# The first feed-forward of a two-model kernel: tile pairs as seven block products in three parts, late modulation units moved to the down parts

## The reference

```python
def swiglu(h, w1, w2):
    gate, up = jnp.split(h @ w1, 2, axis=-1)
    return (jax.nn.silu(gate) * up) @ w2
...
    cond = jax.nn.silu(c)
    for layer in range(DEPTH):
        mod = cond @ ada_w[layer] + ada_b[layer]
        sh1, sc1, g1, sh2, sc2, g2 = jnp.split(mod, 6, axis=-1)
        ...
        h = modulate(rms_norm(x, ffn_norm[layer]), sh2, sc2)
        x = x + g2[:, None, :] * swiglu(h, ffn_w1[layer], ffn_w2[layer])
```

## Time and profile before

| | |
|---|---|
| median of 3 runs | 2526.47 us (2524.81 to 2528.64) |
| the profiled execution's own time | 2526.73 us |
| its span | 2524.7 us |
| mean granted TensorE clock | 0.992 of full speed |
| TensorE, matmuls | 2465.2 us, 98% |
| GpSimd | 1787.9 us, 71% |
| VectorE | 1144.8 us, 45% |
| ScalarE | 542.3 us, 21% |
| first layer's feed-forward, from its first raw tile to the next layer's first shift rows | 362.57 to 740.01 us |
| second layer's, the same stretch | 937.16 to 1293.27 us |

### The profile page before, as it was taken

The page is one execution under the profiler, slowest core; times in us unless marked ns, Lnnn a source line. Parts: engine busy times, 40 slices in busy tenths (PEclk is TensorE's granted clock), DMA queues, the critical chain, the costliest instruction groups (busy, mean ns, idle before and its releaser), DMA issues.

```text
span 2524.7 us, 34103 instructions
## 1 busy us (share of the span) xinstructions
PE 2465.2 (98%) x12183; PEld 1997.5 (79%) x12183; DVE 1144.8 (45%) x2070; ACT 542.3 (21%) x1091; POOL 1787.9 (71%) x1519
## 2 busy tenths in 40 slices
PE   6999999999999999999999999999999999999998
PEld 3677778888887768898988778788878888888886
DVE  5897756444337448363570223105664124331322
ACT  3213520000012522151511011113443101100100
POOL 5564367788887457767798755786555988888885
PEclk9999999999999999999999999999999999999999
DMA  6323225555532122232342211221112222222222
GB/s 260 125 75 134 75 100 178 188 182 173 195 104 75 47 68 92 99 109 93 107 159 97 84 59 59 84 92 67 59 51 101 93 98 92 93 98 100 92 100 83
DMA packets 73376, 267.64 MB, mean 106 GB/s; under 512 B 8240, under 2 KB 9024, under 8 KB 72768
## 3 DMA queue, kind: packets, MB, share of 16 engines
q1 hardware_dynamic: 60288, 215.97, 25.3%
q10 hardware_dynamic: 12992, 50.34, 5.8%
HBM read 262.08 MB, written 4.19 MB: 105 GB/s over the span
## 4 chain that ended last, share of the span: by engine, by line
PE 88%; DVE 6%; POOL 2%; ACT 1%; DMA 1%; issue 1%; ACTq 0%; DVEq 0%; SPq 0%; POOLq 0%
PE ps L444 22%; PE ps L445 22%; PE ps L446 22%; PE ps L845 2%; PE ps L849 2%; PE ps L848 2%; PE ps L675 2%; PE ps L676 2%; PE ps L677 2%; PE ps L1278 1%; PE ps L696 1%; PE ps L1334 1%; POOL lowers L2195 1%; DMA ring<-in_stream 1%; PE ps L1359 1%
## 5 line engine op out<-in xcount | busy, mean ns | idle before, releaser
L2192 POOL TENSOR_TENSOR uppers<-ring,ones 128x512 fp32r<-128x512 f32 x714 | 758.2, 1062 | 562.6 <-DMA ring<-in_stream 558.6
L2195 POOL TENSOR_TENSOR lowers<-ring,uppers 128x512 fp32r<-128x512 f32 x714 | 937.9, 1314 | 55.9
L444 PE MATMUL ps<-x_hi,uppers 128*128 128x512 f32 x864 | 351.5, 407 | 0.0
L446 PE MATMUL ps<-x_hi,lowers 128*128 128x512 f32 x864 | 337.3, 390 | 0.0
L445 PE MATMUL ps<-x_lo,uppers 128*128 128x512 f32 x864 | 337.0, 390 | 0.0
L444 PE MATMUL ps<-h_hi,uppers 128*128 128x264 f32 (+1 forms) x832 | 285.7, 343 | 4.0 <-DVE od_lo L3146 3.4
L445 PE MATMUL ps<-h_lo,uppers 128*128 128x264 f32 (+1 forms) x832 | 279.6, 336 | 0.0
L446 PE MATMUL ps<-h_hi,lowers 128*128 128x264 f32 (+1 forms) x832 | 278.8, 335 | 0.0
L445 PE MATMUL ps<-hid,uppers 128*128 128x512 f32 x704 | 274.3, 390 | 0.0
L444 PE MATMUL ps<-hid,uppers 128*128 128x512 f32 x672 | 263.0, 391 | 0.0
L446 PE MATMUL ps<-hid,lowers 128*128 128x512 f32 x672 | 261.6, 389 | 0.0
(11 more groups left out here) (432 smaller groups left out, 4180.9 us busy)
## 6 DMA issues: line engine op xcount, KB each, us to landing
ring<-in_stream SPq DMA_DIRECT2D x389, 512.0 KB, 3.2
sq<-in_ada_late ACTq DMA_DIRECT2D x20, 512.0 KB, 3.2
rs<-in_ada_late ACTq DMA_DIRECT2D x20, 512.0 KB, 4.7
big<-in_ada_late ACTq DMA_DIRECT2D x16, 512.0 KB, 4.3
big<-in_stream SPq DMA_DIRECT2D x13, 512.0 KB, 16.0
gate<-in_ada_rest ACTq DMA_DIRECT2D x12, 512.0 KB, 3.2
big<-in_ada_rest ACTq DMA_DIRECT2D x12, 512.0 KB, 3.8
hbuf<-in_stream SPq DMA_DIRECT2D x4, 512.0 KB, 6.8
```

Of the source, the lines that this page charges most:

```text
L444: pe.matmul(out, upper, hi, start=start, stop=False)
L446: return pe.matmul(out, lower, hi, start=False, stop=stop)
L2192: pool.tensor_tensor(uppers[:, s, at], w[:, at], ones[:, 0:1].broadcast_to((P, UNIT // 2)), ALU.mult)\
L2195: pool.tensor_tensor(lowers[:, s, at], w[:, at], uppers[:, s, at].bitcast(F32), ALU.subtract)\
```

## The change

The first layer gets the second's form: `ffn` goes on all engines, and `ffn1` takes a layer. All 40 late units move out of the up stage: groups 0 to 4 stand between the residuals of down part a, groups 5 to 9 between those of part b. Their sums stand behind down tiles 1, 2, 4, 5 and 6 of these parts. Their loads are issued by ScalarE as one stretch of 20 ahead of `first_weights` of the next run. Late and last units use the same two buffers in `big`. The four last groups stay ahead of residuals 0 to 3 and their sums behind tiles 1 to 4, now of part c. The second raw operand of f0 and of the next norm moves to other memory; the wait for the last tile's first unit goes, the raw splits stay together ahead of residual 7.

```diff
-        late_w = [sq, rs]
+        LATE0 = 20 * S
...
+        PLAIN = 3
-        HIDDEN_AT = {"f0": 0, "f1": FF}
+        HIDDEN_AT = {"f0": 0, "f1": 2 * PLAIN}
...
+        def late0(k):
+
+            return late_hi[:, k, :], late0_lo[:, k, :]
...
+        LATE_GROUPS = ((0, 1), (2, 3, 4), (5, 6, 7, 8, 9))
+        LATE_SUM_BEHIND = (1, 2, 4, 5, 6)
...
-        last_w = [big[:, TAIL + n * UNIT:TAIL + (n + 1) * UNIT].rearrange("p (a b) -> p a b", b=S) for n in (1, 2)]
+        late_w = last_w = [big[:, TAIL + n * UNIT:TAIL + (n + 1) * UNIT].rearrange("p (a b) -> p a b", b=S) for n in (1, 2)]
...
# TensorE
             def late_sum(i):
+                if i in (0, 2, 5):
+                    claim(7, ("late", [g[0] for g in LATE_GROUPS].index(i)), True)
                 pe.wait_ge(sem("late_read1"), i * 2 + 2)
...
-            def down_part(st, pack, part):
+            def down_part(st, pack, part, behind=None):
...
+                if behind is None:
+                    with pe.Fori(0, 2) as i:
+                        for q in range(4):
+                            tile(i, q)
+                else:
+                    for n in range(KC):
+                        tile(n // 4, n % 4)
+                        behind(n)
+
+            def late_behind(n, first):
+
+                if n in LATE_SUM_BEHIND:
+                    late_sum(first + LATE_SUM_BEHIND.index(n))
+
+            def last_behind(n):
+
+                if 1 <= n <= ADA_LAST:
+                    if n == 1:
+                        claim(7, "late2", True)
+                    ada_sum("last", n - 1, C("chunk_carry"), ps[:, 7, (n - 1) * NT:n * NT])
+
+            def ffn1(st, layer):
+
+                w1, w2 = f"w1_{layer}", f"w2_{layer}"
+                early, late, last = (lambda n: late_behind(n, 0), lambda n: late_behind(n, 5), last_behind) if layer == 0 else 3 * [None]
...
                 seven_products(st, KC - 2 * PLAIN)
-                down_part("f1a", "w2_1", 0)
+                down_part(st + "a", w2, 0, early)
...
-            ffn("f0", 0)
+            ffn1("f0", 0)
...
# ScalarE
+            def late_loads(first, count):
+
+                for unit in range(first, first + count):
+                    if unit >= 2:
+                        act.wait_ge(sem(f"late_read{unit % 2}"), unit // 2)
+                    late_load(unit, unit % 2)
+
             def ffn1(st):
...
                 for run in (1, 2):
+                    if st == "f0":
+                        late_loads(5 * ADA_UNITS * (run - 1), 5 * ADA_UNITS)
                     first_weights(st, run)
                     seven_run(st, run, 0)
...
# VectorE
             def residual(...):
                 for k in range(KC):
+                    if before is not None:
+                        before(k)
                     if between is not None and k == KC - 1:
                         between()
...
-                    if k == KC - 1 and held is not None:
-                        dve.wait_ge(emptied[held % RING], held // RING + 1)
+                    if k == KC - 1 and held:
                         for n in range(KC - 1):
                             raw_split(st, n, *raw(n))
...
+            def late_out(n):
+
+                first, count = LATE_GROUPS[n][0], len(LATE_GROUPS[n])
+                a, at = (ADA_FIRST + ADA_REST + first) * NT, first * NT
+                dve.wait_ge(sem("late_sum_free"), first + count + 1)
+                drain_link(tt(mod[:, a:a + count * NT], ps[:, 7, at:at + count * NT], V("ada_b", a, count * NT), ALU.add), ("late", n))
+
+            def early_groups(k):
+
+                if k == 0:
+                    late_group(0)
+                    late_group(1)
+                    late_out(0)
+                elif 3 <= k < 6:
+                    late_group(k - 1)
+                elif k == 6:
+                    late_out(1)
+
+            def late_groups(k):
+
+                if k in (0, 1, 2, 4, 5):
+                    late_group(5 + (0, 1, 2, 4, 5).index(k))
+                elif k == 6:
+                    late_out(2)
...
+                for run, part, groups in ((1, "a", early_groups), (2, "b", late_groups)):
+                    residual(st + part, None, layer, 5, between=lambda: first_weights(st, run), before=groups if layer == 0 else None)
                     seven_run(st, run, 0)
...
-            residual("f0", "n1", 0, 5, raw=lambda k: (late_hi[:, k, :], late_lo[:, k, :]), held=last_tile["f0"], last=True)
+            residual("f0c", "n1", 0, 5, raw=late0, held=True, last=True)
```

More of the change, by code:

```diff
@@ L783, in late_sum @@
                 mm.then_inc(sem("late_sum_free"), 1)
[L785 to L831, removed]
@@ L900, in down_part, with tile @@
                 done = state["pairs"]
-                with pe.Fori(0, 2) as i:
-                    for q in range(4):
+                def tile(i, q, first=True):
                         take(i, q)
@@ L934, in ffn1 @@
                 seven_products(st, KC - 2 * PLAIN)
-                down_part("f1a", "w2_1", 0)
-                stream("w1_1", 2 * KC, 2 * KC)
+                down_part(st + "a", w2, 0, early)
+                stream(w1, 2 * KC, 2 * KC)
                 seven_products(st, KC)
-                down_part("f1b", "w2_1", 1)
-                stream("w1_1", 4 * KC, 2 * PARTS[2])
+                down_part(st + "b", w2, 1, late)
+                stream(w1, 4 * KC, 2 * PARTS[2])
                 seven_products(st, PARTS[2])
[L941 to L947, removed]
+                if layer == 1:
+                    claim(7, "meta_ss")
+                    pe.wait_ge(sem("meta_squared"), 1)
+                    for k in range(KC):
+                        mm = pe.matmul(ps[:, 7, 0:META], ones[:, :], sq[:, 0, k * META:(k + 1) * META],
+                                       start=k == 0, stop=k == KC - 1)
+                    mm.then_inc(full[7], 1)
+                down_part(st + "c", w2, 2, last)
             def first_mix_out():
@@ L1200, in _ @@
             first_mix_out()
[L1201 to L1205 removed]
+            ffn1("f0", 0)
             stream("cd", 0, 4)
[L1208 removed]
+            raw_tiles("n1", [("u", t) for t in range(4)], late0, True)
             for x in range(2):
@@ L1676, in shift_rows, with ffn_pass @@
                     drain(f(bias_rows[:, p, :], ps[0:2, b, 0:2 * P], ACT.Copy), b)
-            def ffn_pass(st, i, late=0, pairs=(0, 1)):
+            def ffn_pass(st, i, pairs=(0, 1)):
                 if type(i) is int and i == 0:
@@ L2321, in sum_square, with residual @@
                 ins.then_inc(sem("x_summed"), 1)
-            def residual(y, st, layer=None, part=0, raw=None, held=None, rs2=False, last=False, between=None):
+            def residual(y, st, layer=None, part=0, raw=None, held=False, rs2=False, last=False, between=None, before=None):
                 for k in range(KC):
+                    if before is not None:
+                        before(k)
                     if between is not None and k == KC - 1:
@@ L2351, in residual @@
                         continue
-                    if raw is not None and (held is None or k == KC - 1):
+                    if raw is not None and (not held or k == KC - 1):
                         raw_split(st, k, *raw(k))
@@ L2543, in first_pass @@
-            def first_pass(st, late, hid=hid, kept=False):
+            def first_pass(st, hid, kept):
                 layer = 0 if st == "f0" else 1
@@ L2575, in first_pass, with ffn_pass @@
                     normalise(st, k, x_hi[:, k, :], x_lo[:, k, :], coef, shift, kept)
[L2576 to L2579, removed]
                 pair(1)
-                if late:
-                    late_unit(0, 2)
-                    late_unit(0, 3)
-            def ffn_pass(st, i, late, hid=hid, pairs=(0, 1)):
+            def ffn_pass(st, i, hid, pairs=(0, 1)):
                 for p in pairs:
```

77 lines of the change are left out of this document (31 added, 46 removed).

## The result

The changed kernel takes 2595.53 us (median of 4 runs, 2593.46 to 2597.02), the kernel before 2526.42: a ratio of 1.0272, interval 1.0259 to 1.0284. It is 69 us slower; the forecast was 2590, slower by 63. The profiled execution took 2596.24 us, with a span of 2594.3 and a mean granted clock of 0.982 of full speed.

What follows compares the result with a forecast made beforehand. TensorE, busy 98% of the span, was taken to bound the kernel. Terms -11.6 + 34.4 + 28.6 + 4.3 + 7.6 = +63.3 us gave 2590 us, with an 8 in 10 range of 2558 to 2616.

Steps and rivals of the forecast that it cites:

- The pairs: First layer's feed-forward, 16 of 22 pairs in the new form: 163.5 us against 175.1 before, a gain of 11.6 us.
- Parts a and b: Down parts with five late groups each: loads pace units at 2.8 us, parts end at 65.2, costing 34.4 us together.
- Part c: Last down part: four last groups one behind another outlast its shorter tiles, ending at 64.9 us, costing 28.6 us.
- The entry: Entry to the second model layer: raw splits standing together delay residual 7's square, TensorE waits, costing 4.3 us.
- The clock: Lower granted clock behind each down part's last wait and at the second layer's entry: four times 1.9, 7.6 us.
- Rival (1): Late and last loads in the down parts at the lone price, 2.3 us per unit: 2556 to 2563 us; chance 0.13.
- Rival (2): Late and last loads in the down parts at the crowded price, 3.4 us per unit: 2616 us; chance 0.12.
- Rival (3): In the down parts loads cost nothing and VectorE's own 1.55 us per unit decides: 2538 us; chance 0.03.
- (4): In the down parts the groups fit behind the tiles and only the pairs' gain is left: 2515 us; chance 0.05.
- (5): First layer's pairs don't gain, because more waits stand in their runs: 2602 us; chance 0.04.

## Why the prediction was right

It held in direction, range and mechanism: two buffers and the time of a load set the pace of the units, and the parts wait for it. That the total came so close is partly luck, since the parts cost 9.0 us more than forecast and the entry 4.2 less. By its own steps:

- **The pairs**: 163.5 forecast, 20.9 + 81.8 + 61.2 = 163.9 measured. Right.
- **Parts a and b**: 65.2 each forecast, and 1.9 of clock; 71.6 and 69.3 measured. The start was right (first unit at 4.9, forecast 5.3). The pace was 2.92 per unit in part a and 2.82 in part b, forecast 2.8. The row of 2.8 came from one group; with loads of 4.1 and operations of 1.55, (4.1 + 1.55)/2 gives 2.83. So the last sum stood at 61.9 in part a and 60.4 in part b instead of 58.9. The other 3.4 and 2.7 us are the clock.
- **Part c**: 64.9 and 1.9 forecast, 69.2 measured. The last sum came at 789.98 - 738.40 = 51.6; the forecast has it at 51.8. The first group was slower than forecast (its sum at 17.1, where 5.5 + 10.0 was expected; the slowest last load took 7.1), the later ones ran at 11.4, 11.7 and 11.3 instead of 12.1. What was missing is behind the sum: 17.6 us in place of 13.1, of which 1.2 is the wait for GpSimd's lowers ahead of the shift rows, and the rest the clock.
- **The entry**: 4.3 and 1.9 of clock forecast, 1.98 measured. This term was too large. Residual 6 started 64.0 into the part (802.36), 5.2 ahead of the last tile's end, and the last tile ended 4.3 later than forecast (69.2 for 64.9), while the square was ready 2.9 later (815.13 - 738.40 = 76.7 for 73.8) and wanted 5.6 behind the tile instead of 4.6: what delayed the tile hid the splits. The 4.6 was a misreading. The matmuls at 744.65 in the earlier trace rows read `big`; residual 7's square lies in `sq`, and the pair that reads it starts at 745.51, 5.5 behind the tile. By that row the stall would have been forecast at 3.4. Behind the stall of 1.98 the products ran at full rate, and that was luck as well: in the run without arithmetic a stall of 1.95 at the same place was followed by 3.4 us at 0.50.
- **The clock**: four times 1.9 forecast. Behind the three last sums it cost 3.4 (9.63 against 0.81 + 5.44), 2.7 and 3.4 (17.58 less the 1.2 of waiting, against 0.81 + 12.25), 9.5 us together, and nothing at the entry. I had halved the 3.4 us of the earlier trace rows; behind the last sum of part a the clock stays at 1.2 GHz for 6.8 us. The bound of 10 held.

The sum erred by 6.3 us: +9.0 in the three parts, -4.2 at the entry, and 1.5 in small ones (pairs, and the stretches ahead of and behind the stage). Rival (1), a load at the lone price, fell: the median load is 4.1, not 3.1. Rival (2), 3.4 per unit, fell as well. Rival (3) can be read off the run without loads: 2537.19, forecast 2538, with 1 us in part a, none in part b, and 13.9 in part c for the 13.4. Rivals (4) and (5) fell with the parts' waits and the runs' lengths.

## What to carry to other kernels

Work that waits for loads has a pace of its own: (load + compute) / buffers, here (4.1 + 1.55)/2. Before moving such work to another stage, multiply that pace by the units that the stage gets and hold it against the stage's length; the arithmetic alone (20 x 1.55 = 31 us) would have fitted the stage of 48 us. The pace can't fall below the arithmetic, and the load itself gets slower with more of them under way (5.4 us with four). Where the pace was too slow, two more buffers did more here than loads of half the size (2547 against 2574 us), with the DMA engines' share at 0.80; what more than four would do was not tried.

And when a wait appears on TensorE, price the slow piece behind it too: within a stage it only shortens the next wait, and behind the last one it counts in full (3.4, 2.7 and 3.4 us here).

## What the runs showed of the hardware

Waits of TensorE of 0.4 to 1.8 us left the granted clock at 1.00 in parts a and b with four buffers, and all waits of 2.4 us and more in the changed kernel's parts were followed by pieces at 0.5. In between, the length of the wait alone doesn't decide. With half the bytes a wait of 1.75 us, ahead of the last sum of part a, was followed by such a piece too, and of the stalls at the entry that of 1.95 us was in the run without arithmetic, that of 1.98 in the changed kernel was not. The last wait of part a of the changed kernel, 2.86 us after others before it, gave the first of these windows behind it, the 1.75 the second:

```profile
516.50:523.30 6.80, 6.78 (x20) 5.72 (x21) 5.36 (x9) 2.41 (x5) 3.23 (x3) 0.50 0.02 8
...
513.50:516.80 3.30, 3.30 (x10) 2.56 (x9) 3.20 (x6) 1.55 (x3) 2.37 (x2) 0.50 0.02 5
```

The 512 KB loads took 4.1 us with two of them allowed under way beside the stream, and 5.4 with four, while the bytes moved per us rose from 206 to 285 GB/s: the engines had room that two buffers could not use.
